# Two transformer blocks on one NeuronCore: six raw weight tiles through the whole program, three split tiles in place of four, and splits two steps ahead in place of three

## The reference

```python
def first_block(x, ...):                       # D = 2048
    proj = rmsnorm(x) @ w_in                   # 2048 x 6144: q, k, v of two kinds of attention
    ya = dilated_attention(qa, ka, va)         # 8 heads of 128, three masks, one softmax per branch
    yb = diff_attention(qb, kb, vb, lam)       # 8 heads, two softmaxes each, then a norm
    x = x + concat([ya, yb]) @ w_out           # 2048 x 2048
    h = rmsnorm(x)
    x = x + (silu(h @ w_gate) * (h @ w_up)) @ w_down      # 5632 wide
    return rmsnorm(x)

def second_block(x, ...):
    proj = rmsnorm_2(x) @ w_in_2               # 2048 x 11264: retention, attention in blocks, two gates
    merged = sigmoid(g_ret) * (o_ret @ w_ret_up) + sigmoid(g_moba) * (o_moba @ w_moba_up)
    x = x + merged @ w_out_2
    a, b = split(causal_dwconv(rmsnorm_2(x) @ w_ffn_up_2))  # three taps, 2 x 5632 wide
    x = x + (silu(a) * b) @ w_ffn_down_2
    return rmsnorm_2(x)
```

## Time and profile before

| | |
|---|---|
| median of 3 runs | 2539.62 us (2538.71 to 2539.82) |
| the profiled execution, its own time | 2539.04 us |
| its span, first to last instruction | 2537.4 us |
| TensorE busy | 2502.1 us, 99% |
| VectorE busy | 2022.2 us, 80% |
| ScalarE busy | 1360.2 us, 54% |
| bytes read from HBM | 476.57 MB, 189 GB/s over the span |

### The profile page before, as it was taken

The page is one execution under the profiler, slowest core; times in us unless marked ns, Lnnn a source line. Parts: engine busy times, 40 slices in busy tenths (PEclk is TensorE's granted clock), DMA queues, the critical chain, the costliest instruction groups (busy, mean ns, idle before and its releaser), DMA issues.

```text
span 2537.4 us, 28120 instructions
## 1 busy us (share of the span) xinstructions
PE 2502.1 (99%) x11418; PEld 2069.2 (82%) x11418; DVE 2022.2 (80%) x1652; ACT 1360.2 (54%) x1274; POOL 6.2 (0%) x15
## 2 busy tenths in 40 slices
PE   8999999999999999999999999999999999999998
PEld 7787888888888888887888788888888888888886
DVE  6777567788888888869787757777789999999996
ACT  6455555555555555546465555444565555555554
POOL 0000000000000000000000000000000000000000
PEclk9999999999999999999999999999999999999999
DMA  8446456655555555554645546456565555555552
GB/s 282 153 151 211 133 166 199 221 199 199 198 199 199 199 199 199 182 188 149 199 150 198 203 162 215 162 186 233 175 222 197 191 194 198 198 192 192 196 192 92
DMA packets 239615, 480.49 MB, mean 189 GB/s; under 512 B 7632, under 2 KB 7760, under 8 KB 239232
## 3 DMA queue, kind: packets, MB, share of 16 engines
q1 hardware_dynamic: 238496, 474.10, 55.2%
q0 software_dynamic: 992, 4.60, 0.5%
HBM read 476.57 MB, written 2.10 MB: 189 GB/s over the span
## 4 chain that ended last, share of the span: by engine, by line
PE 89%; DVE 6%; issue 2%; ACT 2%; DMA 1%; DVEq 0%; SPq 0%; ACTq 0%
PE acc L733 21%; PE acc L737 21%; PE acc L735 21%; PE misc L733 7%; PE misc L737 7%; PE misc L735 7%; DVE w_lo L1659 3%; PE misc L765 2%; DMA w_raw<-in_w_in 1%; DVE w_raw L1640 1%; ACT w_hi L1180 1%; PE misc L848 0%; DVE x L1749 0%; PE misc L842 0%; PE misc L828 0%
## 5 line engine op out<-in xcount | busy, mean ns | idle before, releaser
L1659 DVE TENSOR_TENSOR w_lo<-w_raw,w_hi 128x2048 fp32r<-128x2048 f32 x432 | 985.2, 2286 | 207.1 <-ACT w_hi L1180 206.0
L1180 ACT ACTIVATE w_hi<-w_raw 128x2048 fp32r<-128x2048 f32 x432 | 827.0, 1917 | 519.9 <-PE acc L737 353.3
L733 PE MATMUL acc<-w_hi,xt_hi 128*128 128x512 f32 x1240 | 490.4, 395 | 8.0 <-ACT qk_stage L1183 4.2
L737 PE MATMUL acc<-w_hi,xt_lo 128*128 128x512 f32 x1240 | 483.8, 390 | 0.0
L735 PE MATMUL acc<-w_lo,xt_hi 128*128 128x512 f32 x1240 | 483.3, 390 | 0.0
L733 PEld LDWEIGHTS acc<-w_hi,xt_hi 128*128 128x128 f32 x1240 | 233.2, 188 | 61.2 <-ACT qk_stage L1183 5.4
L1659 DVE TENSOR_TENSOR w_lo<-w_raw_more,w_hi 128x2048 fp32r<-128x2048 f32 x101 | 230.9, 2286 | 60.4 <-ACT w_hi L1180 60.0
L1180 ACT ACTIVATE w_hi<-w_raw_more 128x2048 fp32r<-128x2048 f32 x101 | 193.6, 1917 | 155.9 <-PE acc L737 84.6
L737 PEld LDWEIGHTS acc<-w_hi,xt_lo 128*128 128x128 f32 x1240 | 233.1, 188 | 49.3
L735 PEld LDWEIGHTS acc<-w_lo,xt_hi 128*128 128x128 f32 x1240 | 233.4, 188 | 46.9
L733 PE MATMUL misc<-w_hi,xt_hi 128*128 128x512 f32 x676 | 264.6, 391 | 0.0
(11 more groups left out here) (312 smaller groups left out, 3414.5 us busy)
## 6 DMA issues: line engine op xcount, KB each, us to landing
w_raw<-in_w_in SPq DMA_DIRECT2D x136, 1024.0 KB, 5.1
w_raw<-in_w_ffn_up SPq DMA_DIRECT2D x60, 1024.0 KB, 5.1
w_raw<-in_w_up SPq DMA_DIRECT2D x33, 1024.0 KB, 5.3
w_raw<-in_w_out SPq DMA_DIRECT2D x32, 1024.0 KB, 5.1
w_raw<-in_w_down SPq DMA_DIRECT2D x30, 1024.0 KB, 6.4
w_raw_more<-in_w_ffn_up SPq DMA_DIRECT2D x28, 1024.0 KB, 5.0
w_raw<-in_w_ffn_down SPq DMA_DIRECT2D x28, 1024.0 KB, 6.3
w_raw<-in_w_gate SPq DMA_DIRECT2D x27, 1024.0 KB, 5.2
```

The costliest lines, as they stand in the source:

```text
L733: nc.tensor.matmul(bank, hi[:, j, :], w_hi[:, t % RING, j, :], start=first and j == 0, stop=False, skip_group_check=shared)
L737: end = nc.tensor.matmul(bank, lo[:, j, :], w_hi[:, t % RING, j, :], start=False, stop=last and j == C - 1, skip_group_check=shared)
L1180: nc.scalar.activation(w_hi[:, t % RING], raw_tile(steps[t].slot), ACT.Copy).then_inc(hi_ready, 1)
L1659: nc.vector.tensor_tensor(w_lo[:, t % RING], raw_tile(steps[t].slot), w_hi[:, t % RING].bitcast(F32), ALU.subtract).then_inc(lo_ready, 1)
```

## The change

`RING` becomes 3, so the rings of `w_hi` and `w_lo` hold three tiles each, and `LEAD`, which is `RING - 1`, becomes 2. The 16 + 16 KB that this frees make room for six raw slots in one place, which hold through the whole program; the two extra slots of the feed-forward networks and the plan's special treatment of them go. Two waits are written anew: the four quarters of x are still loaded ahead of the first four tiles, and POOL fetches the tables of the second block after step P4 of the first `ffn1` iteration instead of when the extra slots are free.

```diff
-RING = 4
+RING = 3
 LEAD = RING - 1
...
-    def load(weight, row, col, release, slots=RING):
-        slot = min(range(slots), key=lambda k: free[k])
+    def load(weight, row, col, release):
+        slot = min(range(RAW_SLOTS), key=lambda k: free[k])
...
     def ffn(which, down_weight, a_weight, a_col, b_weight, b_col):
-        free[RING:] = [len(steps) + 9] * (RAW_SLOTS - RING)
         project(a_weight, [a_col])
         project(b_weight, [b_col])
         for i in range(1, NF):
             with_products(order_of(which, i), a_weight, a_col + i * N, b_weight, b_col + i * N, down_weight,
-                          (i - 1) * N, RAW_SLOTS)
-        more_free[which] = max(free[RING:])
+                          (i - 1) * N)
...
-    raw = place("w_raw", [P, RING, C, N], F32, base)
-    w_hi = place("w_hi", [P, RING, C, N], F32R, base + 32 * KB)
-    w_lo = place("w_lo", [P, RING, C, N], F32R, base + 64 * KB)
+    raw = place("w_raw", [P, RAW_SLOTS, C, N], F32, base)
+    w_hi = place("w_hi", [P, RING, C, N], F32R, base + 48 * KB)
+    w_lo = place("w_lo", [P, RING, C, N], F32R, base + 72 * KB)
...
-    raw_more = place("w_raw_more", [P, RAW_SLOTS - RING, C, N], F32, ph + 40 * KB)
...
     def raw_tile(slot):
-        return raw[:, slot] if slot < RING else raw_more[:, slot - RING]
+        return raw[:, slot]
...
         for k, ld in enumerate(loads):
-            if k < RING:
+            if k < Q:
                 load_x(k)
...
-        pool.wait_ge(lo_ready, more_free[1] + 1)
+        pool.wait_ge(tile_used, STEP[("ffn1", 1), "P4"] + 1)
         load(decay[:], ins["decay"], tables2_loaded)
```

More of the change, by code:

```diff
@@ L178, in plan_weights @@
 def plan_weights():
-    loads, steps, sums, more_free = [], [], {}, {}
+    loads, steps, sums = [], [], {}
     free = [-1] * RAW_SLOTS
     count = [0] * RAW_SLOTS
-    def load(weight, row, col, release, slots=RING):
-        slot = min(range(slots), key=lambda k: free[k])
+    def load(weight, row, col, release):
+        slot = min(range(RAW_SLOTS), key=lambda k: free[k])
         loads.append(Load(weight, row, col, slot, free[slot]))
@@ L202, in down, with with_products @@
             tile(weight, row, n * N)
-    def with_products(order, a_weight, a_col, b_weight, b_col, down_weight=None, down_row=0, slots=RING):
+    def with_products(order, a_weight, a_col, b_weight, b_col, down_weight=None, down_row=0):
         b = len(steps)
@@ L219, in need @@
             if name not in here:
-                here[name] = load(*where[name], release.get(name, at.get(name)), slots)
+                here[name] = load(*where[name], release.get(name, at.get(name)))
             return here[name]
@@ L274, in plan_weights @@
     assert len(steps) == STEPS
-    return loads, steps, sums, more_free
+    return loads, steps, sums
 def plan_pairs():
@@ L615, in build @@
     before = plan_misc_banks()
-    loads, steps, sums, more_free = plan_weights()
+    loads, steps, sums = plan_weights()
     pairs = plan_pairs()
     def raw_tile(slot):
-        return raw[:, slot] if slot < RING else raw_more[:, slot - RING]
+        return raw[:, slot]
     def pair_of(key):
```

## The result

The changed kernel takes 2578.47 us (median of 4 runs, 2577.69 to 2578.88) against 2539.72 for the kernel before (median of 4, 2538.71 to 2541.29): ratio 1.0152, 95% interval 1.0137 to 1.0168. That is 38.8 us slower; forecast was 2570 us, some 30 more than before, with a range of 2551 to 2592.

The account below looks back on a forecast made before the run. TensorE, busy 2502.1 of 2537.4 us, was taken as the bound, so its waits decide. Places summed to +26.0 us and new half-clock stretches to +5.1; with 2539.0 that gave 2570 us, range 2551 to 2592.

Parts of the forecast that it names:

- new half-clock stretches: Clock falls after three of four waits of 3.4 to 5 us in rounds 1, 2, 4, 7: 1.7 each, +5.1.
- The rule by which each place was priced: Everywhere, step s's split ends where s+1's did, shifted 2.28 us by moved sums; lateness plus about 0.1 us is lost.
- k0 of round 4: In round 4, step k0 was to lose 1.9 us.
- U2 of the first `ffn1` iteration: In the first `ffn1` iteration, U2 was to lose 1.1 us, since the norm stands ahead of its split.
- the four that I added up: TensorE's largest wait groups behind its start-up, as read: 5.4, 4.2, 1.2 and 1.0 us, 11.8 us together.
- rival 2: Attention: waits for `qk_stage` and `sig_ret` vanish, splits keep up; 11.8 us and 3.4 of half clock go; 2524 us; chance 0.06.
- Rival 1: Every feed-forward iteration loses, at P3, U2, U3 in `ffn2` and U2 in `ffn1`: 45 + 8 us more, 2620 us; chance 0.11.
- The sum for P6: In `ffn2`, this sum, now behind `conv_a`, was taken as covered by P5, G2 and their 8.2 us: no cost.
- Rivals 2 to 4: Besides rival 2: the third, stalls in one round partly cancel, 2553 us (0.13); the fourth, the change is idle, 2539 us (0.08).

Follow-up runs that it names:

- the experiment on the kernel before: Kernel before (ring of four, three steps ahead), VectorE's reading of a pair's results moved ahead of the split in steps without a softmax piece: 2533.92 us, ratio 0.9981.

## Why the prediction was right, and where its sizes were off

The table gives each place by the ends of its steps in the two traces, profile against profile; each of mine without the +5.1 of new half-clock stretches, which I hadn't given a place.

| place | forecast | measured |
|---|---|---|
| start, round 0 | +1.5 | +0.7 |
| round 1 | +5.1 | +8.3 |
| `down` 0, round 2 | +4.1 | +10.2 |
| round 3, other downs | +5.4 | +7.0 |
| `ffn1` | +2.45 | +2.0 |
| round 4 | +2.7 | +1.7 |
| round 5 | -0.7 | -0.8 |
| round 6 | +1.6 | +1.7 |
| round 7 | +4.0 | +8.8 |
| `merge` | -1.5 | -1.9 |
| `ffn2` | +1.35 | +1.4 |
| new half-clock stretches | +5.1 | (in the rows above) |
| sum | +31.1 | +39.1 |

- **The rule by which each place was priced held.** The waits foretold and measured: G3 of round 1 4.2 and 3.83, P4 2.2 and 2.09, G2 of round 2 5.0 and 5.48, its G3 2.4 and 2.57, D2 of `down` 2 2.2 and 2.74, 235 4.5 and 4.18. 20 waits with 37.9 us stood where 30 with 25 to 40 were forecast.
- **Its reason was only half right.** I wrote that a split can't begin before TensorE has left the slot, and that slot and lead change together. With a fourth slot and `LEAD` 2 nothing came back: the place in the engines' lists decides by itself.
- **The term that was mis-sized is the clock.** The sum has three new stretches of 1.7 us (+5.1) less two old ones (-3.4), +1.7 net. Measured are eight in place of two, 16.5 against 3.4 us of lost work, +13.1 net. Two errors made it: I looked only at waits from 3.4 us up as candidates, where those of 2.1 to 2.7 us at P4, G3 and D2 did it too, and I took each stretch as long as the ones of before, where three after waits of 3.2 to 5.5 us were twice as long. The upper bound that I kept for the term, 7 us, was too low.
- **The rest was too high**, 29.4 without the clock where the difference of the two traces leaves 39.1 - 13.1 = 26.0: of the waits of round 1 that at U3 was 1.4 and not 2.3, k0 of round 4 and U2 of the first `ffn1` iteration didn't wait, and the start lost half. So 11.4 us too little for the clock met 3.4 us too much for the waits. The errors are of opposite sign, and that brought the time 3 us nearer than the clock term alone would have.
- **Readings:** P7 of round 1 doesn't wait, and all of `qk_stage` and `sig_ret` is gone, as written; the experiment on the kernel before shows VectorE's part of these waits to be the split in front of the reading. For ScalarE's part it is shown only that `LEAD` 2 takes it away. The first list of waits was read short: two groups for `v`, 1.7 us each, are larger than two of the four that I added up, so the waits that could go were 15.2 us and not 11.8, and rival 2 would have been 2520 us.
- **The feed-forward networks** lost 0.2 us an iteration, for P5, and nothing at U2 of the first, where 1.1 was forecast: the sums agree in part by chance. Rival 1 is out. VectorE's busy time is the same within 2 us. The sum for P6 was indeed covered.
- **Raw slots:** nothing was taken for them. Beside three split tiles they are worth some 3 us by the ends of the steps, which the clock hid in the time. ScalarE's DMA waits fell from 22.7 us to 0.2, under the 10 forecast.
- **Rivals 2 to 4** fail by the 37.9 us of waits. Of rival 2 its half is true: with w_hi first TensorE waits 5.2 us for splits, the earlier readings show, and the time, 2528, lies near the 2524 that it gave.

The place of the loss, `LEAD`, is shown by an experiment, and so are the price of the clock and the cause of VectorE's reading waits. What decides whether and for how long a wait lowers the clock stays open. For `LEAD` 3 six raw and four split tiles don't fit beside each other, and their worth there wasn't tried.

## What to carry to other kernels

Buffers and lead are two things. Here a ring of three split tiles with six raw ones and one of four with four made no difference, and one step less of lead cost 39 us, since each fill stands behind other work in the list of the engine that does it; compare the end of each fill with the first use of the tile before it. Where an operand comes in two parts, use all of the first part before waiting for the second: it covered up to 3.6 us of lateness a step here and turned a loss of 39 us into a gain of 10. And a wait of TensorE over 2 us is to be priced with the half clock that may stand behind it, here 14 us on 26 of such waits. When two versions lie within some us of each other, compare their half-clock stretches before the times: twice here a difference of 3 us was luck of the clock.

## What the hardware showed

Of the waits of 2 us and more, the changed kernel shows eight (2.08 to 5.48 us), and behind each the granted clock fell to 1.2 GHz, for 3.4 us in five cases and for 6.8 in three. None of its seven waits between 1.0 and 1.5 us did that. It isn't strict, neither between 1.5 and 2 us nor above. In the kernel with w_hi first a wait of 1.88 us at 130.76 was followed by a stretch at half clock, one of 1.77 at 195.9 wasn't; of the waits of before, 2.21 and 2.27 us were and 2.67 wasn't. The wait at G3 of round 7, 3.2 us, was followed by 6.8 us at half clock in the changed kernel and by none in the kernel with four raw slots in the rounds and in the one with the gains moved. In all profiled runs 41 of the 46 waits of 2 us and more (the one for x at the start aside) were followed by half clock. That rule of the Trainium skill ("TensorE: Matmul & The Clock Gate", "HAM oscillation — how this bites in real kernels"), by which waits between bursts re-throttle the engine, was the better guide for the changed kernel: eight of eight, where I had given three. The exceptions above it doesn't cover. Matmuls by zeros in the waits kept the clock at its upper level (0.998 in the mean against 0.991), though they compute nothing.
